# Second layer's modulation moved behind the transposes: scale and shift as columns on ScalarE, the residual's affine after them, one row step fewer

## The reference

```python
for i in range(DEPTH):
    mod = jax.nn.silu(c) @ ada_w[i] + ada_b[i]
    shift, scale, gate = jnp.split(mod[:, None, :], 3, axis=-1)
    u = x * (1 + scale) + shift
    y = mixer_dilated(u, ...) if i % 2 == 0 else mixer_mla(u, ...)
    x = layernorm(DEEPNORM_ALPHA * x + gate * y, ln_g[i], ln_b[i])
```

## Time and profile before

| what | us |
|---|---|
| median of three runs | 4199.13 |
| lowest, highest | 4191.97, 4199.76 |
| profiled execution | 4202.13 |
| its span in the profile | 4200.3 |
| TensorE busy | 3934.5 (94%) |
| VectorE busy | 2182.2 (52%) |
| GpSimd busy | 1890.6 (45%) |
| ScalarE busy | 1408.2 (34%) |
| mean granted clock of TensorE | 0.969 |

### The profile page before, as it was taken

One profiled execution on the slowest core, in us unless ns is written; L12 is line 12 of the kernel. 1 busy time (PEld: TensorE's weight loads), 2 busy tenths in 40 slices (PEclk: granted clock), 3 DMA queues, 4 the chain that ended last, 5 costly groups with the idle time before them and its releaser, 6 DMA issues.

```text
span 4200.3 us, 49747 instructions
## 1 busy us (share of the span) xinstructions
PE 3934.5 (94%) x19191; PEld 3195.1 (76%) x19191; DVE 2182.2 (52%) x3415; ACT 1408.2 (34%) x2906; POOL 1890.6 (45%) x1709
## 2 busy tenths in 40 slices
PE   8999999789999999899888899999998898899998
PEld 4677789678788887787566788888786576788887
DVE  2241323473677774613746877724514737777623
ACT  1120212222666663312543433312213533333311
POOL 1313112073233332622142778888432043788885
PEclk9999999799999999999999999999999999999999
DMA  5312211332100001210022222344310022222453
GB/s 173 113 48 78 63 45 42 99 104 60 32 6 11 6 11 56 101 37 24 1 68 94 78 88 79 124 164 135 107 42 15 1 86 92 82 83 83 154 170 130
DMA packets 248531, 313.62 MB, mean 75 GB/s; under 512 B 39956, under 2 KB 161060, under 8 KB 248296
## 3 DMA queue, kind: packets, MB, share of 16 engines
q1 hardware_dynamic: 214456, 231.87, 17.9%
q10 hardware_dynamic: 33840, 78.58, 5.4%
HBM read 255.12 MB, written 53.15 MB: 73 GB/s over the span
## 4 chain that ended last, share of the span: by engine, by line
PE 71%; DVE 17%; ACT 5%; issue 3%; DMA 1%; POOL 1%; ACTq 0%; SPq 0%; DVEq 0%; POOLq 0%
PE ps L127 68%; PE ps L130 3%; DVE cst_sm L150 3%; DVE ml_p L139 3%; ACT thi L133 1%; DVE tlo L139 1%; DVE f_ta L147 1%; DVE m_hb L147 1%; DVE m_z L147 1%; DVE da_sg L156 1%; ACT m_junk L133 1%; DVE tfl L147 1%; POOL mix_z L139 1%; ACT ml_o L133 1%; DVE f_tb L147 0%
## 5 line engine op out<-in xcount | busy, mean ns | idle before, releaser
L136 POOL CAST whi<-wst 128x512 fp32r<-128x512 f32 (+3 forms) x524 | 406.7, 776 | 1407.1 <-DMA wst<-in_a_w_in 484.5
L139 POOL TENSOR_TENSOR wlo<-wst,whi 128x512 fp32r<-128x512 f32 (+2 forms) x650 | 920.6, 1423 | 46.2 <-ACT whi L133 4.2
L127 PE MATMUL ps<-whi,thi 128*128 128x512 f32 (+3 forms) x1816 | 706.5, 389 | 7.8 <-POOL wlo L139 3.5
L127 PE MATMUL ps<-whi,tlo 128*128 128x512 f32 (+3 forms) x1816 | 693.9, 382 | 0.0
L127 PE MATMUL ps<-wlo,thi 128*128 128x512 f32 (+3 forms) x1816 | 693.8, 382 | 0.0
L127 PEld LDWEIGHTS ps<-whi,thi 128*128 128x128 f32 x1816 | 364.0, 200 | 86.7 <-issue 21.4
L127 PEld LDWEIGHTS ps<-whi,tlo 128*128 128x128 f32 x1816 | 363.8, 200 | 57.4
L127 PEld LDWEIGHTS ps<-wlo,thi 128*128 128x128 f32 x1816 | 364.6, 201 | 55.9
L127 PE MATMUL ps<-thi,whi 128*128 128x512 f32 x856 | 340.0, 397 | 14.6 <-POOL wlo L139 11.1
L127 PE MATMUL ps<-tlo,whi 128*128 128x512 f32 x856 | 338.2, 395 | 0.0
L127 PE MATMUL ps<-thi,wlo 128*128 128x512 f32 x856 | 337.7, 395 | 0.0
(11 more groups left out here) (382 smaller groups left out, 8335.8 us busy)
## 6 DMA issues: line engine op xcount, KB each, us to landing
wst<-in_w_down SPq DMA_DIRECT2D x140, 256.0 KB, 3.2
wst<-in_w_up SPq DMA_DIRECT2D x126, 256.0 KB, 2.9
scr_h<-f_tb SPq DMA_DIRECT2D x44, 512.0 KB, 4.0
wst<-in_w_in SPq DMA_DIRECT2D x64, 256.0 KB, 2.7
wst<-in_a_w_in SPq DMA_DIRECT2D x72, 192.0 KB, 2.4
wst<-in_ada_w SPq DMA_DIRECT2D x48, 256.0 KB, 3.3
tfi<-in_ada_w SPq DMA_DIRECT2D x48, 256.0 KB, 2.6
f_T2lw<-scr_h SPq DMA_DIRECT2D x48, 256.0 KB, 3.8
```

Source lines behind the costliest of these rows:

```text
L127: return self.none if self.e is None else self.e.matmul(*a, **k)
L136: return self.none if self.e is None else self.e.tensor_copy(*a)
L139: return self.none if self.e is None else self.e.tensor_tensor(*a)
```

## The change

- The last step of stage "a" becomes step 2: TensorE turns the normalized `z` itself, so `hb`, its multiply and add, and the folded tile `lt` are gone.
- The new `act_modulated` applies shift and scale while evicting: in the transposed layout they are one value for each partition, so each block of 128x128 is one activation with a column of scale and a column of bias, from PSUM to a new buffer `ta_raw`. A 128x512 copy then gives the high part. VectorE takes the low part from `ta_raw`, in SBUF, not from PSUM.
- The residual's affine comes after the transposes, since it overwrites `z`: on VectorE in the last step for rows 0 to 4, on GpSimd as before for rows 5 to 7, there behind their transposes in the tails. GpSimd has no work for rows 0 to 4. Row j's store is issued with row j + 1's last step, row 7's behind the tails.
- Shift, scale, g and b come as columns of `sm` by 32 small DMAs on SyncE's queue, ahead of the output weights; two of the three broadcasts on ScalarE's queue go. `dve_out` folds the columns with three operations of 8 columns.
- `act_latent` waits for the last normalization, not for the last `hb`.

```diff
-                              hb=[r.new(f"hb{i}", [128, 1024])[:] for i in range(3)])
-        self.lt = r.new("lt", [128, 1024])
+        self.rows["a"] = dict(z=z, g1=lg, g2=lb, xr=[...], hb=[None])
+        self.ta_raw = [r.new(f"tr{i}", [128, 4, 128]) for i in range(2)]
+        self.mcol = [self.sm[:, 384 + 8 * i:392 + 8 * i] for i in range(5)]
...
+        return self.S.at("row_lo", (j, 1)) if st == "a" else self.B.done(("T", st, j, 1))
...
+        sp.wait_ge(*self.S.at("st_m", 5))
+        for dst, src in zip(self.mcol, (self.d_m[0], self.d_m[1], self.I["ln_g"][0], self.I["ln_b"][0])):
+            for k in range(8):
+                sp.dma_start(dst[:, k:k + 1], src[blk(k)].rearrange("(p o) -> p o", o=1)).then_inc(*self.S.up("ld_col", None, 16))
...
-        for n, d in enumerate((self.msh, self.msc, self.gate[1])):
-            q.dma_start(d[:], self.d_m[n].partition_broadcast(128)).then_inc(*S.up("ld_ada", 1, 16))
+        q.dma_start(self.gate[1][:], self.d_m[2].partition_broadcast(128)).then_inc(*S.up("ld_ada", 1, 16))
...
-    TAIL = {"a": 3, "b": 5, "m": 3, "f": 3}
+    TAIL = {"a": 2, "b": 5, "m": 3, "f": 3}
...
+            if kind == "a":
+                if j:
+                    self.act_store(q, st, j - 1)
+                self.act_modulated(q, j)
+                return
...
+    def act_modulated(self, q, j):
+        S, ps = self.S, self.ps
+        q.wait_ge(*S.at("mod_a"))
+        for i in range(2):
+            key, raw = ("T", "a", j, i), self.ta_raw[i]
+            b = self.B.of(key)
+            q.wait_ge(*S.at("turned", key))
+            if j:
+                q.wait_ge(*S.at("row_lo", (j - 1, i)))
+            for k in range(4):
+                ins = q.activation(raw[:, k, :], ps[:, b, blk(k)], ACT.Identity, scale=self.mcol[1][:, 4 * i + k:4 * i + k + 1],
+                                   bias=self.mcol[0][:, 4 * i + k:4 * i + k + 1])
+            ins.then_inc(*self.B.free(key, "evac_a"))
+            q.wait_ge(*self.B.done(key))
+            q.activation(self.thi[:, 4 * i:4 * i + 4, blk(j)], raw[:], ACT.Copy).then_inc(*S.up("hi", key))
...
+                if kind == "a":
+                    t = self.thi[:, 4 * i:4 * i + 4, blk(j)]
+                    q.wait_ge(*S.at("hi", ("T", st, j, i)))
+                    q.tensor_tensor(self.tlo[:, 4 * i:4 * i + 4, blk(j)], self.ta_raw[i][:], t.bitcast(F32), ALU.subtract).then_inc(
+                        *S.up("row_lo", (j, i)))
...
+            if kind == "a" and j < 5:
+                q.wait_ge(*S.at("turned", ("T", st, j, 1)))
+                q.tensor_tensor(z, z, r["g1"][:], ALU.mult).then_inc(*S.up("v_seq"))
+                q.wait_ge(*S.last("v_seq"))
+                q.tensor_tensor(z, z, r["g2"][:], ALU.add).then_inc(*S.up("row_zd", (st, j)))
...
-        if kind == "a" and n == 2 and j < 5:
-            q.wait_ge(*S.at("row_norm", (st, j)))
-            q.wait_ge(*S.at("mod_a"))
-            if j >= 3:
-                q.wait_ge(*S.at("turned", ("T", st, j - 3, 1)))
-            q.tensor_tensor(h, z, self.msc[:], ALU.mult).then_inc(*S.up("row_m", (st, j)))
-        elif (kind == "a" and n == 3) or (kind == "b" and n == 2):
+        if kind in "ab" and n == 2 and (kind == "b" or j >= 5):
             q.wait_ge(*S.at("row_norm", (st, j)))
             q.wait_ge(*S.at("ld_gain", st))
             if kind == "a":
-                q.wait_ge(*S.at("row_m", (st, j)) if j < 5 else S.at("row_mv2", (st, j)))
+                q.wait_ge(*S.at("turned", ("T", st, j, 1)))
...
-        q.wait_ge(*S.at("row_h", ("a", 7)))
+        q.wait_ge(*S.at("row_norm", ("a", 7)))
...
         self.tails(self.act_row, q, "a")
+        self.act_store(q, "a", 7)
```

More of the change, by code:

```diff
@@ L363, in layout @@
         lg, lb = r.new("lg", [128, 1024]), r.new("lb", [128, 1024])
-        self.rows["a"] = dict(z=z, g1=lg, g2=lb, xr=[r.new(f"xr{i}", [128, 1024])[:] for i in range(2)],
-                              hb=[r.new(f"hb{i}", [128, 1024])[:] for i in range(3)])
-        self.lt = r.new("lt", [128, 1024])
+        self.rows["a"] = dict(z=z, g1=lg, g2=lb, xr=[r.new(f"xr{i}", [128, 1024])[:] for i in range(2)], hb=[None])
+        r.off += 8192
+        self.ta_raw = [r.new(f"tr{i}", [128, 4, 128]) for i in range(2)]
+        self.mcol = [self.sm[:, 384 + 8 * i:392 + 8 * i] for i in range(5)]
         r = Region(self, gen, self.end, "mla")
@@ L700, in T_ready @@
     def T_ready(self, st, j):
-        return self.B.done(("T", st, j, 1))
+        return self.S.at("row_lo", (j, 1)) if st == "a" else self.B.done(("T", st, j, 1))
     def pe_start(self, q):
@@ L1342, in pe_row @@
             r = self.rows[st]
-            h = r["hb"][j % len(r["hb"])]
+            h = r["z"][:, j, :] if st == "a" else r["hb"][j % len(r["hb"])]
             for i in range(2):
@@ L1346, in pe_row @@
                              "tq" if self.kind(st) == "m" and j >= 5 else "tr4",
-                             [self.S.at("row_h", (st, j))])
+                             [self.S.at("row_norm" if st == "a" else "row_h", (st, j))])
     def act_row_load(self, q, st, j):
@@ L1366, in act_store @@
         to = self.row_source(st)[1]
-        q.wait_ge(*self.S.at("row_zp" if self.kind(st) in "ab" else "row_z", (st, j)))
+        q.wait_ge(*self.S.at("row_zd" if st == "a" and j < 5 else "row_zp" if self.kind(st) in "ab" else "row_z", (st, j)))
         q.dma_start(self.out[0, blk(j), :] if to is None else self.d_x[to][j], self.rows[st]["z"][:, j, :]).then_inc(
@@ L1456, in dve_row @@
             for i in range(2):
-                self.dve_lo(q, ("T", st, j, i), 4 * i, 4, j)
+                if kind == "a":
[3 more added lines that the diff above has]
+                        *S.up("row_lo", (j, i)))
+                else:
+                    self.dve_lo(q, ("T", st, j, i), 4 * i, 4, j)
+            if kind == "a" and j < 5:
[3 more added lines that the diff above has]
+                q.tensor_tensor(z, z, r["g2"][:], ALU.add).then_inc(*S.up("row_zd", (st, j)))
             return
@@ L1473, in dve_row @@
                 *S.up("row_nb", (st, j)))
[L1474 to L1477, removed]
-                q.wait_ge(*S.at("row_norm", (st, j)))
-                q.wait_ge(*S.at("turned", ("T", st, j - 3, 1)))
-                q.tensor_tensor(h, z, self.msc[:], ALU.mult).then_inc(*S.up("row_mv2", (st, j)))
-                q.wait_ge(*S.at("row_mv2", (st, j)))
-            q.tensor_tensor(h, h, self.msh[:], ALU.add).then_inc(*S.up("row_h", (st, j)))
         elif (kind == "b" and n == 4) or (kind in "mf" and st != ("f", 1) and n == 2):
@@ L1504, in dve_out @@
         if kind == "a":
-            q.wait_ge(*self.S.at("ld_gain", st))
+            q.wait_ge(*S.at("ld_gain", st))
             q.wait_ge(*S.at("ld_ada", 1))
-            q.tensor_tensor(self.lt[:], r["g2"][:], self.msc[:], ALU.mult).then_inc(*S.up("v_seq"))
+            q.wait_ge(*S.at("ld_col"))
+            sh, sc, g, b, t = self.mcol
+            q.tensor_tensor(t, b, sc, ALU.mult).then_inc(*S.up("v_seq"))
             q.wait_ge(*S.last("v_seq"))
-            q.tensor_tensor(self.msh[:], self.msh[:], self.lt[:], ALU.add)
-            q.tensor_tensor(self.msc[:], self.msc[:], r["g1"][:], ALU.mult).then_inc(*S.up("mod_a"))
-            q.wait_ge(*S.at("mod_a"))
+            q.tensor_tensor(sh, sh, t, ALU.add)
+            q.tensor_tensor(sc, sc, g, ALU.mult).then_inc(*S.up("mod_a"))
         for h in range(2):
```

## The result

The changed kernel takes 4210.66 us (median of 5, 4208.94 to 4213.71), the one before, run beside it, 4197.65: a ratio of 1.0034, 95% interval 1.0021 to 1.0048 (the ratio, here and below, is worked out from all executions; the two medians alone give 1.0031). It is slower, by 0.34%. The profiled execution is 4212.06 us with a span of 4210.2, against 4202.13 and 4200.3: +9.9 in the two executions that the traces show, +13.0 between the medians.

What follows compares the result with a forecast made beforehand. TensorE carries 71% of the chain, so only its waits matter; the serial row loop sets the pace. Blocks +9.7, clock +1.5 and affine +5.0 made +16.2; with -1.0 and -3.0, +12.2: median 4199.1 to 4211.3, range 4198 to 4221.

Steps and rivals of the forecast that it cites:

- front: Before the output product: two broadcasts fewer ahead of the softmax sums' load; -3.0 us, ends -4.3 and 0.
- row blocks, to the last eviction: Five serial row blocks of 10.7 us against 9.57, up to the last row's eviction at 925.5; +9.7 us.
- first latent half, clock: After the last eviction: TensorE has stood 6 us and restarts at its lower clock level; +1.5 us (0 to 3).
- affine behind the transposes: After the first latent half: affine of rows 5 to 7 starts only once their transposes have read the row; +5.0 us.
- store of row 7 to gate products: Today's 24.4 us from store to gate products stay, some loads come later against the splits; -1, at most -3.6.
- behind, taken as 0: From 969 on: TensorE runs without a gap, so the delay is passed on in full.
- The columns on SyncE: 32 column loads ahead of the output weights: 14 or 58 us of issuing, costing 0 in both cases.
- rival 1: Row blocks: column operands cost nothing at 128 columns, block 9.3 us, +5 to 4204, no change; chance 0.20.
- The tail: Behind the row blocks: GpSimd's three affine rows take 16.2 us, row 7 affine at 960.7, +16.2, then ScalarE's queue.
- Rival 3: Row blocks: TensorE's clock falls in every block, 14.4 us each if it stays low, +31 to 4230; chance 0.05.
- Rival 4: SyncE's queue: column loads hold up the weights, over 2.9 us an issue, 32 times the excess; with others 0.05.
- Rival 2: Row loop overlaps: block is VectorE's own 7.3 us, faster by 8.3 to 4190.8; chance 0.08.

Runs made afterwards that it cites:

- run of the front alone: Kernel before with the shift and scale broadcasts issued behind the softmax sums and first input rows; 4195.03 us, ratio 0.9999.
- stores last: Changed kernel with the stores of rows 5 to 7 issued behind the squares of the latents; 4208.56 us, ratio 1.0026.
- columns twice: Changed kernel with each of the 32 column loads issued a second time, into unused columns; one execution, 4213.43 us.
- tail on VectorE: Changed kernel with stores of rows 5 to 7 behind the squares and their affine on VectorE, none on GpSimd; 4205.74 us, ratio 1.0012.
- affine of all rows on GpSimd: Changed kernel with the affine of rows 0 to 4 also on GpSimd, behind the transposes; 4198.12 us, ratio 1.0005.
- one plain copy: Changed kernel with each half's four column activations replaced by a plain 128x512 copy, modulation left out; 4200.6 us, ratio 1.0007.
- its order was built: Changed kernel with ScalarE's and VectorE's steps behind a tile in another order, same work; 4187.76 us, ratio 0.9976 to the kernel before.

## Why the prediction was right

4211.3 us were predicted and 4210.7 measured, by the mechanism called likeliest: the row blocks stay serial and grow by ScalarE's small activations, and the affine of rows 5 to 7 moves behind the transposes. That the two times lie 0.6 us apart is luck: executions of one kernel lie further apart, the sum of the terms in the traces is 2.3 us under the one predicted, and the errors of single terms go both ways. The terms, against the two traces:

| term | predicted | measured | from |
|---|---|---|---|
| front | -3.0 | -3.1 | output product at 800.54, then 797.45 |
| row blocks, to the last eviction | +9.7 | +10.0 | 915.80 - 800.54 = 115.26, then 922.71 - 797.45 = 125.26 |
| first latent half, clock | +1.5 | +2.3 | 16.5, then 18.77 |
| affine behind the transposes | +5.0 | +5.1 | 932.30 to 944.46, then 941.48 to 958.77 |
| store of row 7 to gate products | -1.0 | -2.8 | 944.46 to 968.87, then 958.77 to 980.36 |
| behind, taken as 0 | 0 | -1.6 | gate products 23.13, then 21.81; the rest 0.3 |
| sum | +12.2 | +9.9 | |

**The front.** ScalarE's timeline after, against the earlier trace rows:
```profile
764.59 2.43 ACTq L168 DMA_DIRECT2D gt_sa<-scr_y  x3
```
The three issues take 2.43 instead of 5.43: it was the broadcasts that held them, not their own short pieces. Of the 3.1 us, 0.9 lies ahead of the load (765.63 against 766.49), so the part from the load on is 2.2: the load is 2.8 shorter (3.24 on the chain against 6.01), and some 0.5 is lost again, as a later load is now waited for (5.04 of `gt_yr` on the chain at 782.96). The run of the front alone, 2.5 us for this edit, says much the same. Most of the 0.9 lies further ahead, where the two kernels do the same work, so that the term fits by 0.1 is partly chance.

**The columns on SyncE.** 16.5 us for 32, where 14 and 58 were the ends; hidden, and still hidden when they were doubled.

**The row block.** 10.8 where 10.7 was worked out. ScalarE's timeline after, a half of a row:
```profile
877.90 1.50 ACT L133 ACTIVATE mix_tr<-ps,cst_sm 128x128 f32<-128x128 f32 x4
879.43 0.63 ACT L133 ACTIVATE thi<-mix_tr 128x512 fp32r<-128x512 f32 x1
```
A single one takes 0.46, four take 1.50: a step of 0.35, as taken, and both halves are there after 4.23 (4.20). That +179 ns measured on 512 columns hold on 128 was the argument against rival 1, and it held. The Trainium skill ("ScalarE: Activation LUTs", What ACT_TABLE_LOAD costs) gives a step of 0.386 as an estimate; the trace has 0.35, nearer to what the rows of before gave. The last block is 12.01 (predicted 10.7 + 1.6), where the weight splits of GpSimd lie beside VectorE's affine: 1.55 and 1.98 for two passes of 1.2.

**The first latent half.** Of all terms the worst sized among the losses: +2.3 instead of +1.5. TensorE's timeline after:
```profile
922.71 0.71 PE L127 MATMUL ps<-whi,thi 128*128 128x416 f32 x1 [5.00 <-DVE mix_z L139]
...
927.04 0.50 PE L127 MATMUL ps<-whi,thi 128*128 128x416 f32 x1
...
928.32 0.35 PE L127 MATMUL ps<-whi,thi 128*128 128x416 f32 x1
928.51 0.35 PE L127 MATMUL ps<-wlo,thi 128*128 128x416 f32 x1
```
After 5.0 us of standing the products follow each other by 0.35 until 927.4, as at the lower of the two levels (0.85 is the granted clock of 913 to 936), and then by 0.19: 13 products at 0.16 more are 2.1 us. The prediction had TensorE stand 6 us and took 1.5. In three runs with the same work up to here the half took 19.34 (stores last), 19.32 (columns twice) and 18.57 us (tail on VectorE). The wait's length alone does not say what it costs. With the affine of all rows on GpSimd TensorE stood 2.96 us here, and the half took 16.65, as without a loss:
```profile
907.68 0.46 PE L127 MATMUL ps<-whi,thi 128*128 128x416 f32 x1 [2.96 <-DVE mix_z L139]
```
With one plain copy it stood 2.10 and the half took 18.22: its first products followed each other by 0.19, and nine from 912.2 on by 0.35.

The same thing is where the 1.3 us behind the gate products' start come from. The busy table of the kernel before, over the first 6 us from there, and then that of the kernel after:
```profile
969.00:975.00 6.00, 6.00 (x22) 4.77 (x21) 5.70 (x28) 5.84 (x29) 0.00 (x0) 0.78 0.02 4
```
```profile
981.00:987.00 6.00, 6.00 (x28) 4.96 (x27) 5.69 (x28) 5.83 (x30) 1.90 (x2) 1.00 0.02 4
```
Before, TensorE had waited 3.19 and 1.72 us for VectorE's scaling ahead of its last eight transposes, and the first 6 us have a mean clock of 0.78; after, it comes out of a half without a wait and has 1.00. The prediction had said that TensorE is without a gap from there on and that the delay is passed on in full. The first is so (25.0 of 25 us busy from 969 to 994 before, 23.0 of 23 from 981 to 1004 after), and the second leaves out that the gate products begin at another clock.

**The tail.** Three rows of affine in 16.2 us (942.53 to 958.74), as taken, and row 7's store at 958.77 ("near 958"). The 16.2 was the value of the kernel before carried over; here it is made of one pass of 2.35 and five of 2.7 to 2.8, with the low parts between them. The way named, ScalarE's queue, was there, but it was not the only one: the run with the stores last showed that the contention between GpSimd and the low parts gives the same delay without it. The prediction held both in hand, the queue as the mechanism and the port as the reason for an upper bound, but did not see that the second alone is enough.

**The store to the gate products.** The term that was mis-sized most: -2.8 instead of -1.0, within the bound of -3.6. It was taken that VectorE's scaling goes on setting the end, in its company of weight splits. What the chain shows is TensorE's own way: row 7's low part, 19.07 of products and 1.94 of turns. That way was worked out as 20.8 and took 21.6. The scaling had become shorter as well, 20.8 us from the store of row 7 to its end where it was 23.2. VectorE's timeline after, its last operation on the latents:
```profile
979.48 0.11 DVE L165 MEMSET ml_lat<- 128x64 f32 x1
```
It ends at 979.59, some 0.3 us before the last four turns need it (an estimate: 12 of the 16 turns of 1.94 from 978.42). So the two ways end almost together; in the run with the stores last it was VectorE's that ended last.

**The rivals.** Rival 1 fell with the 0.46. Rival 3 (the clock low in every block) did not come: the granted clock is 0.91 over the blocks where it was 0.97, and the time is nowhere near 4230. The clock is a part of the price only, behind the blocks. Rival 4 fell with the doubled loads. Rival 2 did not come in this order and was right as a sum: where its order was built, the block was 7.13 (7.3 worked out) and the time 4187.8 (4190.8).

What stays open: the medians lie 13.0 apart and the profiled executions 9.9. Single executions of one kernel lie some microseconds apart (4189.9 to 4205.5 in 29 of the kernel before), and the table explains only the two that were recorded. By what rule TensorE's clock falls is open too; the terms for it are read from rows.

## What to carry to other kernels

- Before taking work from an engine, look at the chain of waits of one turn of the loop. Where engines wait for each other in a ring, what counts is the sum of the links and not the load of the busiest engine. A cheap test is to put each engine's steps of a turn in another order, so that none waits for what was made last; here that was worth 22.9 us, with no instruction changed.
- If a wait has two causes, taking away one can show nothing. Read what the engine does in the run without the first cause, and take away the second as well, before the theory is dropped.
- An operation that now reads its input from SBUF instead of PSUM may have the same length by itself and another one beside a busy GpSimd.

## What the runs showed of the hardware

- Low parts with both inputs in SBUF (0.69 us alone) took 2.6 each beside GpSimd's affine, in alternation with its passes, which rose from 2.35 to 2.7 to 2.8. Low parts that read one input from PSUM kept their length beside such a pass (1.29 us for two, pass of 2.40).
- Four activations of 128x128 with a column of scale and one of bias take 1.50 us, one plain activation of 128x512 takes 0.60.
- Three issues of the load of the sums took 5.43 us with three broadcasts ahead of them and 2.43 with one. The DMA share was 0.79 to 1.15 in each microsecond from 765 to 770 before, and 0.90 and 1.21 from 765 to 767 after, then 0.60; the last issue ended at 770.6 and at 767.0. So the queue was held while the DMA engines were full.
- A column of 128 values of four bytes took SyncE 0.47 to 0.56 us to issue, a whole broadcast of 512 KB 0.45 to 0.47 on ScalarE's queue.
- After a wait of 5.0 us TensorE's products followed each other at 0.35 us at first and at 0.19 from 927.4 on, which cost 2.1 us; in another run a wait of 2.96 us at the same place cost nothing. Without a wait ahead of them the gate products had a granted clock of 1.00 in their first 6 us instead of 0.78 and took 1.3 less.
